# Rotary rotation in an attention front: a TensorE product against ScalarE copies of 32-row blocks

## What is computed

```python
def rope(x, positions):
    half = x.shape[-1] // 2
    inv = ROPE_THETA ** (-jnp.arange(half, dtype=jnp.float32) / half)
    ang = positions.astype(jnp.float32)[..., None] * inv
    cos = jnp.cos(ang)[:, :, None, :]
    sin = jnp.sin(ang)[:, :, None, :]
    ...
    return jnp.concatenate([x1 * cos - x2 * sin, x2 * cos + x1 * sin], axis=-1).astype(x.dtype)

    q = rope(rms_norm(q, q_gain), positions)
    k = rope(rms_norm(k, k_gain), positions)
    qi = rope(qi, positions).astype(jnp.float32)
    ki = rope(ki, positions)[:, :, 0, :].astype(jnp.float32)
    ...
        logits = jnp.einsum('bqhd,bsd->bqhs', qib, ki) * IDX_DIM ** -0.5
        score = jnp.einsum('bqh,bqhs->bqs', wib, jax.nn.relu(logits))
        _, idx = lax.top_k(score, topk)
```

## Time and profile before

| | us |
|---|---|
| median of 3 runs | 3953.45 (3949.91 to 3955.57) |
| the profiled execution | 3951.66 |
| its span in the trace | 3949.9 |
| the stage `attention_front` in it | from 2316.2 to 2588.5: 272.3 |
| PE busy in that stage | 265.95 |

### The profile page before, as it was taken

The page is one execution under the profiler, slowest core; times in us unless marked ns, Lnnn a source line. Parts: engine busy times, 40 slices in busy tenths (PEclk is TensorE's granted clock), DMA queues, the critical chain, the costliest instruction groups (busy, mean ns, idle before and its releaser), DMA issues. The chain is left out here.

```text
span 3949.9 us, 47449 instructions
## 1 busy us (share of the span) xinstructions
PE 3429.3 (87%) x20913; PEld 1659.7 (42%) x20913; DVE 1110.8 (28%) x1920; ACT 598.7 (15%) x1165; POOL 8.0 (0%) x40
## 2 busy tenths in 40 slices
PE   6988998879988777777777899989999976999998
PEld 3567786334444222222222243454444434444443
DVE  1256655232022000000000024762666014122210
ACT  2133231110021000000000021142221003121100
POOL 0000000000000000000000000000000000000000
PEclk8999999979996999999999999999999987999999
DMA  6234534101220799999999711102333225112120
GB/s 225 70 109 152 192 126 164 57 22 53 75 92 0 325 428 427 426 428 427 425 427 427 330 47 43 64 22 60 121 129 123 93 62 202 64 64 85 64 91 32
DMA packets 222226, 668.71 MB, mean 169 GB/s; under 512 B 31048, under 2 KB 95036, under 8 KB 171205
## 3 DMA queue, kind: packets, MB, share of 16 engines
q1 hardware_dynamic: 221032, 665.31, 43.5%
q10 hardware_dynamic: 989, 0.36, 0.0%
HBM read 640.97 MB, written 22.31 MB: 168 GB/s over the span
## 5 line engine op out<-in xcount | busy, mean ns | idle before, releaser
L2489 PE MATMUL banks<-h_T,weight_ring 128*128 128x512 f32 x1408 | 614.1, 597 | 5.9 <-PEq L89 5.9
L1928 PE MATMUL banks<-weight_ring,xe_T 128*64 128x512 f32 x2048 | 470.2, 601 | 139.2 <-DMA weight_ring<-in_exp_w 136.7
L2489 PEld LDWEIGHTS banks<-h_T,weight_ring 128*128 128x128 f32 x1408 | 268.0, 192 | 338.7 <-issue 338.6
L1928 PEld LDWEIGHTS banks<-weight_ring,xe_T 128*64 128x64 f32 x2048 | 143.4, 137 | 455.5 <-issue 257.9
L1714 PE MATMUL banks<-weight_ring,ffn_act 128*128 128x512 f32 x704 | 307.2, 599 | 14.5 <-PEq L2639 7.5
L1943 PE MATMUL banks<-weight_ring,hid_T 128*64 128x512 f32 x1024 | 235.5, 602 | 80.6 <-DMA weight_ring<-in_exp_w 79.7
L2548 DVE SCALAR_TENSOR_TENSOR conv<-banks,cols,conv 128x510 f32<-128x510 f32 (+1 forms) x176 | 131.8, 749 | 342.2 <-ACT conv L2518 337.5
L1714 PEld LDWEIGHTS banks<-weight_ring,ffn_act 128*128 128x128 f32 x704 | 135.4, 193 | 186.3 <-issue 186.3
L1997 DVE TENSOR_TENSOR hid<-silu,banks 128x1024 f32<-128x1024 f32 x16 | 19.5, 1221 | 654.5 <-issue 561.6
L587 PE MATMUL banks<-h_T,weight_ring 128*128 128x512 f32 x416 | 184.9, 604 | 4.4 <-PEq L89 4.4
L1943 PEld LDWEIGHTS banks<-weight_ring,hid_T 128*64 128x64 f32 x1024 | 71.3, 137 | 244.1 <-issue 141.4
(11 more groups left out here) (548 smaller groups left out, 3707.1 us busy)
## 6 DMA issues: line engine op xcount, KB each, us to landing
weight_ring<-in_exp_w SPq DMA_DIRECT2D x192, 2048.0 KB, 11.0
weight_ring<-in_ada_w SPq DMA_DIRECT2D x24, 2048.0 KB, 8.4
weight_ring<-in_ffn_w_up SPq DMA_DIRECT2D x44, 1024.0 KB, 6.9
weight_ring<-in_mod_w SPq DMA_DIRECT2D x12, 2048.0 KB, 8.5
weight_ring<-in_ffn_w_down SPq DMA_DIRECT2D x10, 2048.0 KB, 7.8
weight_ring<-in_attn_w_in SPq DMA_DIRECT2D x7, 2048.0 KB, 7.7
weight_ring<-in_w_in SPq DMA_DIRECT2D x6, 2048.0 KB, 10.0
weight_ring<-in_w_in SPq DMA_DIRECT2D x9, 1024.0 KB, 5.2
```

Source lines behind the costliest of these rows:

```text
L1928: mm = pe.matmul(k.ps[64 * half:64 * half + 64, 2 * c + b % 2, :], xeT[:, kt, e * CAP:(e + 1) * CAP], w[:, r, 512 * b:512 * b + 512], star ...
L2489: mm = pe.matmul(k.ps[:, b + c, :], w[:, c, kt, m * P:m * P + P], hT[:, kt, :], start=kt == 0, stop=kt == 7)
```

## The change

The product with `rot` is gone from PE's stream. In its place ACT, as soon as it has evicted job s, copies the tile's four blocks of 32 partitions into a new buffer `crossed`, exchanged in pairs (0 to 31 with 32 to 63, 64 to 95 with 96 to 127). Before them it waits for its own eviction to be complete, and, since `crossed` has two halves, for DVE to have finished with the tile before the last. DVE multiplies `crossed` with `sin` in place of the PSUM bank. The sign is put into `sin` once, by one DVE instruction at the start. Since banks 2 and 3 are free, projections go round over four banks, and PE waits for the eviction of job s-4 in place of that of job s-2. ACT gives ring chunks 0 and 1 back in turn 4 and no longer in turn 3.

```diff
+    misc[:, 10] = np.where(q % 64 < 32, -1.0, 1.0)
...
+        crossed = sb("crossed", [P, 2, L])
...
                 job = jobs[s]
-                if s >= 2:
-                    pe.wait_ge(evacuated, s - 1)
-                out = k.ps[:, s % 2, :]
+                if s >= 4:
+                    pe.wait_ge(evacuated, s - 3)
+                out = k.ps[:, s % 4, :]
...
                     pe.wait_ge(evacuated, s)
-                    if r >= 2:
-                        pe.wait_ge(roped, r - 1)
-                    pe.matmul(k.ps[:, 2 + r % 2, :], k.sq("rot"), tile[job], start=True, stop=True).then_inc(rotated, 1)
                     if job[0] == "k":
...
-                    src = k.ps[:, s % 2, :]
+                    src = k.ps[:, s % 4, :]
...
                     if s == 3:
                         act.activation(wi[:], wi_sums, ACT.Copy, scale=IDX_HEADS ** -0.5).then_inc(wi_done, 1)
+                    if s == 4:
                         act.sem_inc(k.ring.used, 1)
                         act.sem_inc(k.ring.used, 1)
                     elif s in (8, 12, 16, 20, 24, 28):
                         act.sem_inc(k.ring.used, 1)
+                    if s + 1 in rope_at:
+                        r = rope_at[s + 1]
+                        act.wait_ge(evacuated, s + 1)
+                        if r >= 2:
+                            act.wait_ge(roped, r - 1)
+                        for p0, p1 in ((0, 32), (32, 0), (64, 96), (96, 64)):
+                            ins = act.activation(crossed[p0:p0 + 32, r % 2, :], tile[job][p1:p1 + 32], ACT.Copy)
+                        ins.then_inc(rotated, 1)
                 for n in units_at(s):
...
             dve.wait_ge(tables, 1)
+            link(dve.tensor_scalar(sin[:], sin[:], k.misc[:, 10:11], None, ALU.mult))
             dve.wait_ge(wi_done, 1)
...
-                    link(dve.tensor_tensor(tmp[:], k.ps[:, 2 + r % 2, :], sin[:], ALU.mult))
+                    link(dve.tensor_tensor(tmp[:], crossed[:, r % 2, :], sin[:], ALU.mult))
```

## The result

The changed kernel takes 3957.16 us in the median of 20 runs (3947.67 to 3967.36), the kernel before 3952.27 (3945.18 to 3957.08, also 20 runs). The ratio is 1.0015, with a 95% interval of 1.0008 to 1.0022: 0.15% slower, about 5 to 6 us. The forecast was 3.9 us faster, with a range of 3942 to 3956, and it was wrong in sign. The profiled execution of the changed kernel took 3963.85, its span 3962.0.

A forecast was written before the change was run, and what follows sets the result against it. PE's stream was taken to bound the stage: 12.9 us saved in ordinary turns, less 3.9 for later relus and 5.1 for clock falls, makes 3.9 us faster, 3953.45 - 3.9 = 3949.5 us, range 3942 to 3956.

The forecast's parts named there:

- What bounds the stage: The changed stage lasts as long as PE's stream, so only what PE issues or waits for counts.
- the ordinary turns: 15 of the 21 turns with a `rot` product: PE doesn't wait for the copies, 15 x 0.86 = 12.9 us saved.
- Edits at nothing: Four banks, the `sin` pass, later chunk release, ACT's waits and the stage's end: no gain or loss.
- The mechanism in the block turns: Six turns where copies precede relus: PE's third logit waits for the first relu, and the clock may fall.
- The price of a copy: ACT's copies of 32 partitions, 512 columns: 0.52 us from start to start, with 0.31 and 0.68 as ends.
- the loss by the relus: Six block turns: relus 0.86, 0.65 and 0.44 us later by width, twice each, 3.9 us lost.
- The lower end of the range: Block turns, copies at 0.31: relus start where they did, all 21 products saved, 18.1 us; as a rival, chance 0.06.
- The clock: PE's six new idle times of 2.1 to 2.3 us in block turns: three falls at 1.7 us, 5.1 us lost.
- The second one: Block turns: PE waits, clock falls nearly each time; 1.2 us slower, 3954.6; chance 0.17 including copies up to 0.68.
- The first rival: Block turns: the clock doesn't fall; 9.0 us faster, 3944.5; chance 0.27 for no fall or one.
- The range: Whole kernel: 3944.5 less 2.5 of spread to 3954.6 plus 1, 3942 to 3956, without dear copies and free relus.
- copies of 0.68 with all six falls: Block turns, dearer copies and a clock fall in each: 5.2 - 10.2 = 5.0 us slower, 3958.5.

The follow-up runs named there:

- relus-first run: Changed kernel with ACT's four copies put behind the relus of the same turn instead of ahead; 3932.86 us, 0.9952 of the kernel before.
- run with two banks: Changed kernel with projections over two banks again and ring chunks 0 and 1 given back in turn 3; 3955.07 us, 1.0011 of the kernel before.
- that with three copies: Changed kernel with the fourth copy left out in the six block turns, result wrong; 3951.63 us, 1.0002 of the kernel before.
- run with two copies: Changed kernel with the four copies replaced by two in other forms, none crossing partitions, and the rotation left out; one execution took 3943.10 us.

## Why the prediction was wrong, point by point

- **What bounds the stage, and the ordinary turns: right.** 15 times 0.86 us were saved. The relus-first run shows the same 0.86 for the six block turns as well.
- **Edits at nothing: right.** The banks and the release cost nothing (279.4 against 279.5), DVE stays ahead of PE at the end, and the later stages kept the shift: 18 us of stage came out as 19 of run time in the relus-first run. PE's last product ends 2.55 us behind DVE's last operation in the changed kernel (2597.51 against 2594.96), as in the kernel before (2.5).
- **The mechanism in the block turns: right.** The relus start behind the copies and PE waits for them at the third logit, six times, and the clock then falls. Both were in the sum. Two of its terms were too small, the clock's by 9.0 us and the relus' by 2.8.
- **The price of a copy: 0.52 taken, 0.64 measured.** It lay inside the bounds (0.31 to 0.68). I read 0.52 from two passes over all 128 partitions, which overlap by 0.1 us. The copies don't overlap, since each begins on another block. Four copies at 0.12 us more, in six turns, make the loss by the relus 6.7 us and not 3.9, and the idle times are 0.35 us longer. The lower end of the range was wrong in another way: with copies of 0.31 in front of them the relus would start at T+2.67, as before, so the six block turns would save little, and not all 21 products. The 18.1 us need relus that start earlier than before, as they do in the relus-first run.
- **The clock: the step that failed.** "I take the middle, three: 5.1 us lost" became six falls and 14.1 us, by two errors. The first is the count: even at 1.8 to 2.0 us of idle time five of six fell. I had put the six idle times between a row in which 2.63 us made it fall and one in which 2.12 us between dense products didn't, and gave the second as much weight as the first. The row that was most like the new place, 2.12 us with 64-row products around it and a fall, was there too, and should have led. Six falls at my price would have been 10.2 us. The second is the price: the earlier trace rows showed a fall of 1.7 us, and I took it for the only size. Three of the six did cost 1.7; the other three stretches at 1.2 GHz lasted twice as long, 6.8 us, and cost 2.8 to 3.2 each.
- **The rivals.** The second one, PE waits and the clock falls nearly each time, is what happened. It was priced at 1.2 us slower, or 5.0 with copies of 0.68, and had a chance of 0.17, copies of up to 0.68 included. With the measured terms it gives 12.9 - 6.7 - 14.1 = 7.9 us slower in the stage; the runs say 4.9 by the medians. The profiled execution is the second slowest of its 20, and how many falls the others had isn't known. That its 5.0 lies so close to the 4.9 is luck, since its falls were priced 3.9 us too low. The first rival, and with it the Trainium skill's rule that pauses this short leave the clock alone (TensorE: Matmul & The Clock Gate, under "Why this matters for your kernels"), is refuted for this place: in the profiles of the change, of the run with two banks and of that with three copies there are 18 pauses of 1.80 to 2.65 us, and 17 of them were followed by the 1.2 GHz level.
- **The range** reached to 3956 and the median is 3957.2. It would have held the time, had each bound been carried through: copies of 0.68 with all six falls stood in the text as 3958.5 and were left out. The 1.2 us by which the median lies outside make the miss look smaller than it was: in the stage the sum was off by 11 us.

## What to carry to other kernels

Work that is taken off the bounding engine and given to a helper must be placed by what that engine waits for next in the helper's order: the same four copies shortened the stage by 18 us behind the relus and lengthened it by 7 ahead of them. A pause of two us on PE can cost more than itself, since the products behind it may run at half the clock. Until a row with the same surroundings shows otherwise, price every new pause of that size with a fall, and a long one. Where a pause can't be avoided, needed work that stands just ahead of it on the same engine is best moved into it.

## What the runs showed of the hardware

- ACT overlaps two successive instructions by about 0.1 us when they begin on the same partition (0.53 us from start to start for 512 columns), and not when the second begins on another (0.64). The number of partitions, 32, 64 or 128, and a shift between input and output made no difference to it.
- With 64-row products and one of 16 columns around it, a pause of PE of 2.44 to 2.65 us was followed by a stretch at 1.2 GHz 12 times in 12 (the change and the run with two banks), of 1.80 to 2.01 us 5 times in 6, of 1.38 to 1.60 us once in 6, and of 1.16 to 1.38 us once in 6 (the run with two copies). In the kernel before and with the relus first, pauses of 0.47 to 0.68 us at the same place never were, in 12.
- Such a stretch lasted either about 3.4 us or about 6.8. In the profiles of the change and of the run with two banks the order was the same in both: long, short, short, long, short, long. What decides it wasn't tried. In all 19 falls of the five profiles, though, the 8 long stretches began between 0.8 us before the end of the pause and 0.4 us behind it, and the 11 short ones 0.6 to 1.7 us behind it.
- 18 products whose result isn't used, put into the six pauses, made the kernel 12 us faster than the change.
